# A two-block transformer kernel: the last mixer pass turns its tokens in two bank pairs, and five passes take their sums of squares from high and low parts

## What is computed

```
h = rms_norm(x, mix_norm_g)
dq, dk, dv, bq, bk, bv, z = split(h @ w_in)
dq, dk = rms_norm over each head of 64 of dq, dk   # sum of squares, root, gain
a = diff_attention(dq, dk, dv, lam)                # 4 head pairs, all keys
bq, bk = rms_norm over each head of 64 of bq, bk
b = dilated_attention(bq, bk, bv)                  # 8 heads, three window patterns
y = concat(a, b) * silu(z)
x = x + y @ w_out
x = x + sigmoid(rms_norm(x) @ w_ple_gate) * (p @ w_ple_proj)
```

## Time and profile before

| | |
|---|---|
| median of 3 runs | 2904.7 us (2899.4 to 2905.01) |
| the profiled execution's own time | 2902.29 us |
| its span, first to last instruction | 2900.5 us |
| PE, PEld busy | 2757.6 us (95%), 2112.9 us (73%) |
| DVE, ACT, POOL busy | 1714.0, 1047.3, 935.8 us |
| mean granted clock of PE | 0.985 of full speed |
| the mixers phase in the span | from about 1893 to 2715 us |

### The profile page before, as it was taken

One profiled execution on the slowest core, in us unless ns is written; L12 is line 12 of the kernel. 1 busy time (PEld: TensorE's weight loads), 2 busy tenths in 40 slices (PEclk: granted clock), 3 DMA queues, 4 the chain that ended last, 5 costly groups with the idle time before them and its releaser, 6 DMA issues. The chain is left out here.

```text
span 2900.5 us, 39452 instructions
## 1 busy us (share of the span) xinstructions
PE 2757.6 (95%) x15534; PEld 2112.9 (73%) x15534; DVE 1714.0 (59%) x2674; ACT 1047.3 (36%) x1735; POOL 935.8 (32%) x549
## 2 busy tenths in 40 slices
PE   6999999999999899999999999979999999998999
PEld 5979797977878677777776887755666666666777
DVE  5787878785021344444455114766676677777586
ACT  4342524343010233233333002345666654444232
POOL 2232323232664122122122334542222143432465
PEclk9999999999999899999999999999999999999999
DMA  4241423233533111110112324421101111113544
GB/s 166 56 88 66 87 73 80 74 81 137 183 109 102 38 52 46 51 48 30 52 45 106 109 73 165 156 93 43 40 19 43 41 44 37 37 44 102 183 149 112
DMA packets 113751, 236.53 MB, mean 82 GB/s; under 512 B 9120, under 2 KB 52896, under 8 KB 113568
## 3 DMA queue, kind: packets, MB, share of 16 engines
q1 hardware_dynamic: 63312, 172.14, 18.2%
q10 hardware_dynamic: 50256, 61.87, 7.3%
HBM read 189.88 MB, written 44.11 MB: 81 GB/s over the span
## 5 line engine op out<-in xcount | busy, mean ns | idle before, releaser
L79 PE MATMUL psum<-u_h,w_hi 128*128 128x512 f32 (+2 forms) x2624 | 1011.1, 385 | 23.8 <-DVE u_h L2874 6.0
L80 PE MATMUL psum<-u_h,w_hi 128*128 128x512 f32 (+2 forms) x2624 | 967.6, 369 | 0.0
L81 PE MATMUL psum<-u_h,w_lo 128*128 128x512 f32 (+2 forms) x2624 | 966.5, 368 | 0.0
L135 POOL TENSOR_SCALAR w_hi<-w_raw 128x1024 fp32r<-128x1024 f32 x212 | 240.7, 1135 | 1469.0 <-ACTq L1324 518.6
L79 PEld LDWEIGHTS psum<-u_h,w_hi 128*128 128x128 f32 x2624 | 497.3, 190 | 155.4 <-issue 68.3
L137 POOL TENSOR_TENSOR w_lo<-w_raw,w_hi 128x1024 fp32r<-128x1024 f32 x212 | 545.9, 2575 | 17.7
L81 PEld LDWEIGHTS psum<-u_h,w_lo 128*128 128x128 f32 x2624 | 497.1, 189 | 71.5
L80 PEld LDWEIGHTS psum<-u_h,w_hi 128*128 128x128 f32 x2624 | 497.6, 190 | 69.5 <-issue 8.9
L2544 ACT ACTIVATE a_exp<-a_exp 128x1024 f32<-128x1024 f32 x96 | 101.6, 1059 | 154.9 <-DVE a_exp L2703 77.6
L1349 ACT ACTIVATE f_exp<-psum 128x1024 f32<-128x1024 f32 (+4 forms) x112 | 82.1, 734 | 192.9 <-PE psum L1207 94.0
L1445 DVE CUSTOM_DVE_ANT_0 f_junk<-psum,f_decay,f_max 128x512 f32<-128x512 f32 (+2 forms) x96 | 60.3, 666 | 133.9 <-PE psum L1230 120.6
(11 more groups left out here) (431 smaller groups left out, 4425.1 us busy)
## 6 DMA issues: line engine op xcount, KB each, us to landing
w_raw<-in_w_all SPq DMA_DIRECT2D x212, 512.0 KB, 3.5
sums_rows<-s_acs ACTq DMA_DIRECT2D x32, 512.0 KB, 8.7
f_decay<-s_nc SPq DMA_DIRECT2D x16, 520.0 KB, 5.6
s_y<-conv_out ACTq DMA_DIRECT2D x16, 512.0 KB, 3.0
yo_raw<-s_y ACTq DMA_DIRECT2D x8, 1024.0 KB, 9.3
x_tok<-in_x SPq DMA_DIRECT2D x8, 512.0 KB, 8.0
s_xT<-xT SPq DMA_DIRECT2D x8, 512.0 KB, 4.9
s_pssd<-fox_last ACTq DMA_DIRECT2D x16, 256.0 KB, 2.2
```

The costliest lines, as they stand in the source:

```text
L79: nc.tensor.matmul(out, w_hi[:, k], a_hi, start=(k == 0 and first), stop=False)
L80: nc.tensor.matmul(out, w_hi[:, k], a_lo, start=False, stop=False)
L81: return nc.tensor.matmul(out, w_lo[:, k], a_hi, start=False, stop=(k == kk - 1 and final))
L135: self.nc.gpsimd.tensor_scalar(self.hi[:, r], self.raw[:, r], 1.0, 1.0, ALU.mult, ALU.mult).then_inc(self.hi_done, 1)
```

## The change

**Sums of squares.** For q = 0 to 4 (`halved(q)`) POOL splits the squares into a high and a low part (`squares_low`), into the buffer `tok`, and PE takes two fp32r products with an fp32r copy of the matrix (`exact`, made once by DVE) instead of one fp32 product. POOL does this at the start of the row in which the projection group ends, ahead of `split_rows` and `W.split` of that row. For q = 1 to 4 the items S of Q0 and Q1 move behind the second projection step of their row (`is_late`).

**Last pass.** Both parts of `p` are turned in row 0, the second through the banks at MX + 512 and OB; `high_p` and `low_p` of both stand in row 1, and the first values product (`spread`, u = 0) waits for the low parts. Embeds start in row 3, one a row. D of the first half moves from row 13 to 11 and D of both halves goes to the bank MX, so that it no longer waits for `copy_out`; `invert` and `finish` of the first half move to rows 12, 13 and 14; ACT copies D of pass 6 ahead of the exponentials of row 0. After the last row embeds 13 and 14 stand ahead of D. `W.split(35)` stands behind the split of `w_ple`. In the closing product, k = 7 of u = 0 comes after two steps of u = 1 instead of four.

```diff
-    is_late = lambda p, x, it: it[0] == "E" and x == 6 or ...
+    is_late = lambda p, x, it: it[0] == "S" and 0 < it[1] <= DIFF and it[2] in (GQ0, GQ1) or it[0] == "E" and x == 6 or ...
+    halved = lambda q: q <= DIFF
-        if x == 13 and p >= 0 and not diff(p):
+        if x == (11 if p == PASSES - 1 else 13) and p >= 0 and not diff(p):
             out.append(("D", p, 0))
...
-            return MX if x < 9 else OB
+            return MX if x < 9 or p == PASSES - 1 else OB
-        placed[("D", PASSES - 1, 1)] = OB + 512
+        placed[("D", PASSES - 1, 1)] = MX
-        TURN_AT, PLE_AT = {0: 0, 2: 1}, {x: [0, 1] if x == 4 else [x - 3] for x in range(4, U)}
+        PLE_AT = {x: [x - 3] for x in range(3, U)}
+        turn_bank = lambda k, h: GB + 512 * h if k == 0 else (MX + 512, OB)[h]
...
+            def squares_low(q, g):
+                c = number_of(q, g)
+                high, low = (tok[:, i, 512 * (c % 2):512 * (c % 2) + 512] for i in range(2))
+                pool.wait_ge(sq_ok, c + 1)
+                nc.gpsimd.tensor_copy(high, sq[:, c % 2]).then_inc(low_ok, 1)
+                pool.wait_ge(low_ok, 2 * c + 1)
+                nc.gpsimd.tensor_tensor(low, sq[:, c % 2], high.bitcast(F32), ALU.subtract).then_inc(low_ok, 1)
...
                 for x in range(U):
+                    for g, k in share(q, x) if q < PASSES and halved(q) else []:
+                        if k == KT - 1 and g <= GQ1:
+                            squares_low(q, g)
                     if q < PASSES and x in normed_at(q):
                         split_rows(q, normed_at(q)[x])
...
-                    elif x == 0:
+                    elif x == 0 and p < LAST:
                         W.split(pool, 0, 0, 4 * p + 7)
...
-            W.split(pool, 0, 0, 36)
+            for n in (35, 36):
+                W.split(pool, 0, 0, n)
...
                 if kind == "D":
-                    pe.wait_ge(o_ok, 2 * q + g + 1)
+                    if placed[it] != MX:
+                        pe.wait_ge(o_ok, 2 * q + g + 1)
...
                 if kind == "S":
-                    pe.wait_ge(sq_ok, number_of(q, g) + 1)
-                    last = nc.tensor.matmul(bank, K.pairs[:, :], sq[:, number_of(q, g) % 2], start=True, stop=True)
+                    c = number_of(q, g)
+                    if halved(q):
+                        pe.wait_ge(const_ok, 1)
+                        pe.wait_ge(low_ok, 2 * c + 2)
+                        for i in range(2):
+                            last = nc.tensor.matmul(bank, exact, tok[:, i, 512 * (c % 2):512 * (c % 2) + 512], start=(i == 0), stop=(i == 1))
+                    else:
+                        pe.wait_ge(sq_ok, c + 1)
+                        last = nc.tensor.matmul(bank, K.pairs[:, :], sq[:, c % 2], start=True, stop=True)
...
+                    if p == LAST:
+                        pe.wait_ge(p_lo_ok, 4)
...
-                    if p == LAST and x in TURN_AT:
-                        turn_p(TURN_AT[x])
+                    if p == LAST and x == 0:
+                        turn_p(0)
+                        turn_p(1)
...
-            extra(("D", PASSES - 1, 1))
-            for n in range(13, 2 * KT):
-                embed(n)
+            for n in (13, 14):
+                embed(n)
+            extra(("D", PASSES - 1, 1))
+            embed(15)
...
-            for u, ks in ((0, range(LAST)), (1, range(4)), (0, [LAST]), (1, range(4, KT))):
+            for u, ks in ((0, range(LAST)), (1, range(2)), (0, [LAST]), (1, range(2, KT))):
...
-                    if p >= 0 and not diff(p) and x in (14, 15):
-                        invert(p, 0, x - 14)
+                    if p >= 0 and not diff(p) and x - (12 if p == LAST else 14) in (0, 1):
+                        invert(p, 0, x % 2)
```

More of the change, by code:

```diff
@@ L2394, in turn_p @@
                 pe.wait_ge(p_got, 32)
[L2395 to L2396 removed]
+                if k == 0:
+                    pe.wait_ge(gfree, 8 * PASSES)
                 for c in range(CH):
[L2398 removed]
+                    at = turn_bank(k, c // 4) + P * (c % 4)
+                    last = nc.tensor.transpose(ps[:, at:at + P], p_in(c)[:, P * k:P * (k + 1)], K.ident[:, :])
                 last.then_inc(pturn, 1)
@@ L2606, in high_p @@
                 for h in range(2):
-                    nc.scalar.activation(p_hi(k, h), ps[:, GB + 512 * h:GB + 512 * h + 512], ACT.Copy).then_inc(p_hi_ok, 1)
+                    nc.scalar.activation(p_hi(k, h), ps[:, turn_bank(k, h):turn_bank(k, h) + 512], ACT.Copy).then_inc(p_hi_ok, 1)
             def high_mix(k):
@@ L2643, in _ @@
                             serve(it)
-                    if p == LAST and x - 1 in TURN_AT:
-                        high_p(TURN_AT[x - 1])
+                    if p == LAST and x == 0:
+                        serve(("D", LAST - 1, 1))
+                    if p == LAST and x == 1:
+                        high_p(0)
+                        high_p(1)
                     if p == LAST and x - 1 in PLE_AT:
@@ L2669, in _ @@
             copy_out(PASSES - 1, 1)
+            for n in (13, 14):
+                take_ple(n)
             serve(("D", PASSES - 1, 1))
-            for n in range(13, 2 * KT):
-                take_ple(n)
+            take_ple(15)
             high_mix(LAST)
@@ L2860, in _ @@
             dve.wait_ge(cleared, 1)
+            nc.vector.tensor_copy(exact, K.pairs[:, :])
             for j in range(2):
@@ L2907, in _ @@
                         root_step(p, 0)
-                    if p >= 0 and x == (14 if diff(p) else 15):
+                    if p >= 0 and x == (14 if diff(p) or p == LAST else 15):
                         finish(p, 0)
@@ L2921, in _ @@
                         low_mix(MIX_AT[x])
-                    if p == LAST and x - 1 in TURN_AT:
-                        low_p(TURN_AT[x - 1])
             for part in range(2):
```

21 lines of the change are left out of this document (12 added, 9 removed).

## The result

The changed kernel takes 2931.6 us (median of 4 runs, 2927.9 to 2933.4) against 2902.7 (2899.4 to 2905.0): the ratio is 1.0094, with a 95% interval of 1.0081 to 1.0107, so 28.9 us or 0.9% slower. Forecast were 2920 and a range of 2903 to 2932. The profiled executions are 2933.4 and 2902.3 us, their spans 2931.6 and 2900.5.

A forecast was written before the change was run, and what follows sets the result against it. PE's stream was taken to bound the passes, while the last pass has 15 us of holes. Opening 12 + passes 15 - last pass 10 = 17 us on 2902.3 gives 2919; median put at 2920, range 2903 to 2932.

The forecast's parts named there:

- The product: PE's sums of squares: two fast products take about 0.55 us instead of 0.95, saving 0.4 each, twenty times, four in the opening.
- The opening: Before pass 0: squares' splits ahead of weight splits on POOL delay V0, Q1 and the first keys; loses 12 us.
- The passes: Passes 0 to 3: delays at K1 and Q0 lose 15 us (11 to 18), the 16 savings of 0.4 included.
- the step on K1: In each pass, PE waits for POOL's split of K1's squares; scores of row 4 start 0.9 us later, savings included.
- The chain through ACT's late copy of Q0: Rows 4 to 7 of each pass: copy waits for K0's split, 4.6 us late; keys then 3.3 to 4.7 late.
- The last pass: Earlier turns and embeds and the new closing order gain 4 + 6 = 10 us (7 to 12).
- The front: Last pass up to the last values product: earlier turned halves and embeds, a lead of 4 us.
- DVE's low parts done at about 2645.5, the first embed at 2646.6: Start of the last pass, both halves turned by about 2641; of the 6.3 us some 5 are left by row 6.
- rival 3: Last pass: late `mix` loads and D in row 11 hold ACT and DVE, only 5 us gained; 2925, chance 0.15.
- Rival 1: Whole kernel: splits are hidden and the fast products pay, V0 starting at 1909; 2887, chance 0.08.
- rival 2: Passes: look-ahead row covers Q0's chain, only K1's 0.9 is lost each time; 2910, chance 0.17.
- Rival 4: Passes: POOL and DVE block each other, 16 pairs holding DVE 0.61 us add 10; 2930, chance 0.10.

The follow-up runs named there:

- direct: Squares' part alone on the kernel before, without POOL's split: ACT writes rounded squares, PE multiplies them twice, low part left out; 2895.4 us, ratio 0.9979.
- passes_only: The kernel before with the squares' part in passes 0 to 3 only, the opening keeping its fp32 product; 2922.8 us, ratio 1.0074.
- weights_first: As squares_only, but in the opening POOL's split of the squares stands behind the weight split of the same row; 2927.3 us, ratio 1.0087.
- k1_late: As squares_only, but S of K1 in q = 1 to 4 stands behind two projection steps of its row; 2929.3 us, ratio 1.0093.
- keys_first: As squares_only, but in row 4 of the passes POOL splits K0's rows ahead of Q0's squares; 2929.9 us, ratio 1.0094.
- pool_only: As squares_only, but S is the one fp32 product again and POOL's two operations stay in place, their output unread; 2931.4 us, ratio 1.0106.
- last_only: The kernel before with the change of the last pass alone, squares again one fp32 product; 2897.2 us, ratio 0.9984.
- end_only: The kernel before with only the last pass's closing part: embeds 13 and 14 ahead of D, D in `MX`, closing order; 2892.4 us, ratio 0.9965.
- squares_only: The kernel before with the squares' part of the change alone, its last pass unchanged; 2937.5 us, ratio 1.0128.

## Why the prediction was right, and where its sizes were off

The direction and the order of the terms were right, the size only just: the measured 2931.6 lies 0.4 us inside the upper bound, and the loss is 28.9 us where the sum gave 17. 2 us of the distance from 2920 are hidden by the baseline, 2904.7 there and 2902.7 in this comparison. That it fell inside is luck: the two large misses, in the passes and the last pass, go the same way, and two of the four runs (2933.2 and 2933.4) lie above the bound.

**The product** (0.4 us, sixteen times): right in the sum, 6.5 us in direct, but not for each: nothing at K0, 0.2 at K1, the rest at Q0 and Q1.

**The opening** (+12): 13.1 by the stages, 14.8 by passes_only. The mechanism is shown by weights_first, which takes 9.1 of it back by order alone (10.3 by the medians). V0 was 6.2 late where 5.1 was said, Q1 14.0 where 13.2. The pairs took 2.5 us here rather than 1.95.

**The passes** (+15, 11 to 18): 21.7, outside its bounds. This is the term that was mis-sized, and what it put at nothing is the clock. By its own count a pass should lose 3.8, 3.8, 3.8 and 3.4. Pass 0, without a stretch at the lower clock, lost 4.2; the other three lost 5.5, 5.3 and 6.7, and 7 us in them stand as PE's busy time and not as a wait. 21.7 less these 7 is the 15 of the forecast. The prediction had reckoned with just such a fall in the opening, and not here. Within pass 0 the step on K1, "Loss 0.9, both savings included", is short as well: counted from S of K0, the scores of row 4 start 9.65 us behind it (2032.87) where it was 8.12, so 1.5 late. The wait is as said, 1.67; most of the two savings of 0.4 is missing, as the pair of K0 takes 0.96 us to the next start, no less than the fp32 product's 0.95, and that of K1 0.63. k1_late, which takes this wait away, gets 7.7 us back in the four passes, 3.5 of them busy time. The chain through ACT's late copy of Q0 is there (counted from S of K0 the copy is 5.2 us late where 4.6 was said, then the logs, the exponentials, the turn). That it starts at that copy is shown by keys_first for the waits at the turn and the values, and pool_only shows that it needs no wait of PE for the low parts. Its last link, the 1.58 before the scores of row 7, stayed in keys_first, where a held DVE step takes the copy's place, so there it is read from the rows. S of Q1, for which the prediction named no wait, waits another 0.6.

**The last pass** (-10): 4.6 by the stages, 4.7 by last_only. The end is as forecast, 6 us, and gives 1.5 more behind the phase, which was not foreseen. The front was to give 4 and costs 1.4. The step that failed is "DVE's low parts done at about 2645.5, the first embed at 2646.6", 9.3 and 10.4 us behind D of pass 6. In the changed kernel they are done 11.2 us behind it, and the first values product, which waits for them, starts 11.5 and ends 13.5 behind it: the first embed comes at 13.4, a lead of 3.3 us on the old order instead of 6.3. 1.7 are left ahead of the wait for `mix`. DVE just ahead of the low parts:

```profile
2676.07 2.56 DVE L2850 COPY a_biased<-a_exp 128x512 f32<-128x512 f32 x1 [1.30 <-ACT a_exp L2573]
2678.67 1.28 DVE L2849 TENSOR_TENSOR a_biased<-a_biased,a_exp 128x384 f32<-128x384 f32 x1
2679.87 2.36 DVE L2850 COPY a_biased<-a_exp 128x128 f32<-128x128 f32 x1
2682.15 2.47 DVE L2721 TENSOR_TENSOR u_h<-psum,u_h 128x512 fp32r<-128x512 f32 x4
```

and POOL beside it:

```profile
2675.97 2.38 POOL L2244 TENSOR_TENSOR u_h<-a_sq,u_h 128x1024 fp32r<-128x1024 f32 x1
...
2679.62 2.52 POOL L137 TENSOR_TENSOR w_lo<-w_raw,w_hi 128x1024 fp32r<-128x1024 f32 x1
```

A copy of 128x512 takes 2.56 us next to POOL's difference (2675.97 + 2.38), and a copy of 128x128 takes 2.36 next to the weight difference (2679.62 + 2.52), which the change moved to just here. In end_only, whose front is the old one, it is the sum between them that is held:

```profile
2635.71 0.67 DVE L2840 COPY a_biased<-a_exp 128x512 f32<-128x512 f32 x1 [1.12 <-ACT a_exp L2567]
2636.42 2.60 DVE L2839 TENSOR_TENSOR a_biased<-a_biased,a_exp 128x384 f32<-128x384 f32 x1
2638.95 1.05 DVE L2840 COPY a_biased<-a_exp 128x128 f32<-128x128 f32 x1
```

From the first copy's start to the end of the three it is 6.1 us here (2676.07 to the next start at 2682.15) and 4.2 there (2635.71 to 2639.92): 1.9 more, which is the 1.9 by which the low parts missed the 9.3. So one more hold by POOL is what this step had left out. This is read from the rows; no kernel was made that moves the weight split alone. The second part of the loss, the 2.39 us before the first `mix` embed, is the wait of rival 3; how much of it comes from ACT and how much from DVE, no run parts. D of the first half in row 11 waits 1.35, less than the forecast's 2.

**The rivals.** Rival 1 is refuted (V0 is 6.2 late), rival 2 too (passes_only). Rival 3 came true in size (4.6 where it said 5), in part by another cause. Rival 4, that POOL and DVE hold each other up in the passes at the price of 10 us, is refuted as a cause of the loss: DVE's busy time fell. But the mechanism exists, at single places: in the last pass's front, and in keys_first, where DVE's busy time in the passes is 286 us instead of squares_only's 275 at the same POOL work. The time of 2931.6 is rival 3's 2925 and 7 us of the passes.

**Sum by the stages:** 2.3 ahead of the phase + 13.1 + 21.7 + 0.1 in passes 4 to 6 - 4.6 - 1.5 behind the phase = 31.1, the difference of the spans. The 2.3 lie in code that runs ahead of the change; without them it is 28.8, beside 28.9 between the medians.

## What to carry to other kernels

Work moved to an idle engine is priced by what stands behind it in that engine's order, not by the engine's busy share: here 20 pairs of operations on an engine busy a quarter of the time turned 6.5 us gained into 35.6 lost, and 28 of these came back by three changes of order (passes and opening still lose 7). When a wait is added to a stream that was full, add to its length the stretch at the lower clock behind it, and look for it in the busy time. Of a change with several parts, time each alone: one part of this one, the end of the last pass, is worth 8.3 us without the rest, and the squares are worth 6.5 only if nobody has to split them.
